# Two blocks on one core: the last VectorE chunk of the conditioning product moved into the feed forward's first up steps, the late pieces started one place earlier, the preparation's TensorE order restored

## The reference, cut to what matters

```python
def first_block(x, mem, ...):
    # rms_norm, projection, window attention + rwkv7 + memory attention
    x = x + concatenate([out_a, out_b, out_m], axis=-1) @ w_out[l]
    x = x + conv_ffn(rms_norm(x, ffn_norm_g[l]), w_up[l], conv_w[l], conv_b[l], w_down[l])

def second_block(x, c, w_ada, b_ada, ...):
    c_act = jax.nn.silu(c)
    mod = c_act @ w_ada[l] + b_ada[l]                 # 1024 x 6144: "conditioning"
    sh1, sc1, g1, sh2, sc2, g2 = jnp.split(mod, 6, axis=-1)
    h = rmsnorm(x, norm1_g[l]) * (1.0 + sc1) + sh1
    proj = h @ w_in[l]                                # queries and keys get a rotary turn
    ...                                               # two attentions, gates, w_out
    x = x + g1 * (merged @ w_out[l])
    h2 = rmsnorm(x, norm2_g[l]) * (1.0 + sc2) + sh2
    x = x + g2 * hierarchical_moe(h2, ...)            # 32 experts, 2 of them per token
```

## Time and profile before

| | us |
|---|---|
| median of the runs shown | 1062.68 |
| the profiled execution, its own time | 1064.43 |
| its span | 1062.6 |
| TensorE matmuls busy | 914.6 (86%) |
| VectorE busy | 551.4 (52%) |
| ScalarE busy | 358.7 (34%) |
| GpSimd busy | 76.1 (7%) |
| mean granted clock of TensorE | 0.944 |

### The profile page before, as it was taken

One profiled execution on the slowest core, in us unless ns is written; L12 is line 12 of the kernel. 1 busy time (PEld: TensorE's weight loads), 2 busy tenths in 40 slices (PEclk: granted clock), 3 DMA queues, 4 the chain that ended last, 5 costly groups with the idle time before them and its releaser, 6 DMA issues.

```text
span 1062.6 us, 19426 instructions
## 1 busy us (share of the span) xinstructions
PE 914.6 (86%) x8462; PEld 708.9 (67%) x8462; DVE 551.4 (52%) x1020; ACT 358.7 (34%) x699; POOL 76.1 (7%) x113
## 2 busy tenths in 40 slices
PE   9999999999999999999999998667665765657885
PEld 8777778489999888998989965334333343334532
DVE  4775688768888757798867543211112121112211
ACT  5710355156776545455553341000001010000002
POOL 3021710000000000331010000000000000000000
PEclk9999999999999999999999999989788788889978
DMA  9545353775554565886549899999999999999994
GB/s 346 168 140 188 144 210 105 261 253 169 164 163 171 204 226 206 266 246 204 179 157 391 348 389 429 428 429 428 430 428 429 428 427 430 429 428 429 427 431 175
DMA packets 76716, 316.21 MB, mean 298 GB/s; under 512 B 4088, under 2 KB 28065, under 8 KB 64209
## 3 DMA queue, kind: packets, MB, share of 16 engines
q1 hardware_dynamic: 71972, 302.24, 72.5%
q0 software_dynamic: 4512, 12.62, 3.9%
q10 hardware_dynamic: 140, 0.04, 0.0%
HBM read 311.72 MB, written 1.06 MB: 294 GB/s over the span
## 4 chain that ended last, share of the span: by engine, by line
PE 58%; DMA 26%; DVE 9%; issue 3%; ACT 2%; ACTq 0%; SPq 0%; POOL 0%; DVEq 0%
PE ps L486 56%; DMA w<-in_w_up 19%; DMA w<-in_w_gate 6%; DVE sp L1937 1%; DMA w<-in_w_ada 1%; DMA rot<-q 1%; PE ps L612 1%; PE ps L2800 1%; DVE w L1041 0%; DVE w L1003 0%; DVE acc L1003 0%; ACT hts L2934 0%; DVE rot L2308 0%; DVE q L2309 0%; DVE q L2311 0%
## 5 line engine op out<-in xcount | busy, mean ns | idle before, releaser
L486 PE MATMUL ps<-w,xg 128*32 128x256 f32 x2016 | 159.3, 475 | 96.9 <-DMA w<-in_w_up 74.1
L486 PE MATMUL ps<-hb,sp 128*128 128x256 f32 x1824 | 225.9, 285 | 0.0
L486 PEld LDWEIGHTS ps<-hb,sp 128*128 128x128 f32 x1824 | 220.1, 190 | 3.0 <-issue 2.5
L486 PEld LDWEIGHTS ps<-w,xg 128*32 128x32 f32 x2016 | 85.0, 132 | 169.1 <-issue 145.0
L1937 DVE TENSOR_TENSOR sp<-w,sp 128x1024 fp32r<-128x1024 f32 x122 | 144.7, 1221 | 38.6 <-ACT sp L1928 38.5
L1928 ACT ACTIVATE sp<-w 128x1024 fp32r<-128x1024 f32 x122 | 122.3, 1052 | 47.4 <-PE ps L486 46.2
L3010 DVE TENSOR_TENSOR cst<-ps,cst 64x256 f32<-64x256 f32 x31 | 13.3, 427 | 218.0 <-ACT cst L2921 218.0
L2921 ACT ACTIVATE cst<-ps 64x256 f32<-64x256 f32 x31 | 11.7, 377 | 313.2 <-PE ps L486 313.2
L3036 DVE TENSOR_TENSOR ost<-ps,cst 32x256 f32<-32x256 f32 x120 | 50.5, 420 | 102.5 <-PE ps L486 99.7
L486 PE MATMUL ps<-w,hts 128*32 128x256 f32 x1024 | 62.8, 386 | 11.9 <-ACT hts L2934 10.3
L486 PE MATMUL ps<-sp,ab 128*128 128x512 f32 x264 | 61.8, 395 | 0.0
(11 more groups left out here) (431 smaller groups left out, 1306.2 us busy)
## 6 DMA issues: line engine op xcount, KB each, us to landing
w<-in_w_down SPq DMA_DIRECT2D x36, 2048.0 KB, 35.8
w<-in_w_gate SPq DMA_DIRECT2D x32, 2048.0 KB, 28.1
w<-in_w_up SPq DMA_DIRECT2D x31, 2048.0 KB, 32.7
w<-in_w_in SPq DMA_DIRECT2D x13, 2048.0 KB, 9.9
w<-in_w_up SPq DMA_DIRECT2D x22, 1024.0 KB, 6.6
w<-in_w_ada SPq DMA_DIRECT2D x8, 2048.0 KB, 8.8
w<-in_w_out SPq DMA_DIRECT2D x4, 2048.0 KB, 8.2
w<-in_w_ada POOLq DMA_DIRECT2D x8, 768.0 KB, 5.6
```

What stands on the lines that cost most here:

```text
L486: return q.eng.matmul(o, l, r, start=start, stop=stop, skip_group_check=True)
```

## The change

It has three parts.

1. **Chunk 7.** `ada_ve(q, 7)` no longer runs between the additions of half 0. Its first four instructions stand behind the split of up half 2, the other four behind each of the next four splits (`up_ve`, i < 2). The activation blocks are numbered by `at_ab(n) = (n + 16) % 22`, so that the first six of them do not lie in slot 6.
2. **Late pieces.** `down_ve` begins with a `next(late_ada)`. GpSimd's program is as it was.
3. **Preparation.** On TensorE the head sums (`hsum_pe`) stand ahead of projection pair 3 and not within it; the sums' spread (`kk_pe`) and both halves of `feat_pe` (16 transposes) stand ahead of pair 4 and not within it.

```diff
+        def at_ab(n):
+            return (n + 16) % 22
...
-        def up_ve(q):
+        def up_ve(q, seventh):
             e = q.eng
             for i in range(11):
...
                 for z in range(2):
                     split_ve(q, 2 * i + z + 3)
+                    if i < 2:
+                        next(seventh, END)
...
         def down_ve(q, late_ada):
+            next(late_ada)
             for j in range(25, 33):
                 split_ve(q, j)
...
-            for i in (6, 7):
-                for _ in ada_ve(q, i):
-                    pass
-                wout_ve(q, 0, (i - 6,))
+            for _ in ada_ve(q, 6):
+                pass
+            wout_ve(q, 0)
+            seventh = ada_ve(q, 7)
...
             split_ve(q, 2)
-            up_ve(q)
+            two(seventh)
+            two(seventh)
+            up_ve(q, seventh)
...
+            hsum_pe(q, 0, HSB, [bsv[:, i, :] for i in range(3)], "hs", (s["r_kk"], 2))
             gates = lora_pe(q, 2)
             for n, _ in enumerate(rpair_steps(q, 3)):
-                if n == 1:
-                    hsum_pe(q, 0, HSB, [bsv[:, i, :] for i in range(3)], "hs", (s["r_kk"], 2))
                 if n in (1, 3, 5):
                     next(gates, END)
-            last = rpair_steps(q, 4)
             rq_pe(q, 0)
-            two(last)
             kk_pe(q)
-            for h in range(2):
-                two(last)
-                feat_pe(q, 1, Xm, lambda i: (s["ht1"], i + 5), hs=(h,))
-            two(last)
+            feat_pe(q, 1, Xm, lambda i: (s["ht1"], i + 5))
+            rpair_pe(q, 4)
```

More of the change, by code:

```diff
@@ L2018, in up_sc @@
                 q.wait_ge(s["u_v"], 9 * i + 9)
-                e.activation(ap_[0][:, 2 * i:2 * i + 2, :], Uc[:, 0:2, :], ACT.Copy).then_inc(s["a_hi"], 1)
-        def up_ve(q):
+                e.activation(ap_[0][:, at_ab(2 * i):at_ab(2 * i) + 2, :], Uc[:, 0:2, :], ACT.Copy).then_inc(s["a_hi"], 1)
+        def up_ve(q, seventh):
             e = q.eng
@@ L2035, in up_ve @@
                 q.wait_ge(s["a_hi"], i + 1)
-                e.tensor_tensor(ap_[1][:, 2 * i:2 * i + 2, :], Uc[:, 0:2, :], ap_[0][:, 2 * i:2 * i + 2, :].bitcast(F), SUB).then_inc(s["a_lo"], 1)
+                e.tensor_tensor(ap_[1][:, at_ab(2 * i):at_ab(2 * i) + 2, :], Uc[:, 0:2, :], ap_[0][:, at_ab(2 * i):at_ab(2 * i) + 2, :].bitcast(F), SUB).then_inc(s["a_lo"], 1)
         def ft3(i):
@@ L2051, in part @@
                         inside()
-                    t = mm3(q, psum[DB[2 * h + z]], [p[:, n, 128 * h:128 * h + 128] for p in ap_], [p[:, k, :] for p in w], n == 0, n == 21)
+                    t = mm3(q, psum[DB[2 * h + z]], [p[:, at_ab(n), 128 * h:128 * h + 128] for p in ap_], [p[:, k, :] for p in w], n == 0, n == 21)
                 return t
```

## The result

| | before | after |
|---|---|---|
| median of the runs, us | 1062.68 (five runs, 1060.68 to 1064.59) | 1094.17 (five runs, 1093.57 to 1096.69) |
| the profiled execution, its own time / its span | 1064.43 / 1062.6 | 1094.17 / 1092.4 |
| TensorE matmuls busy | 914.6 (86%) | 918.6 (84%) |
| mean granted clock | 0.944 | 0.935 |

The ratio is 1.0298, 95% interval 1.0286 to 1.0311: by this ratio the change makes the kernel 31.7 us slower. The forecast was 1088, in a range of 1076 to 1098. The mechanism was the one forecast; the sum was 6 us short.

What follows compares the result with a forecast made beforehand. The prediction took the experts' weight stream (DMA share nine tenths) to bound the kernel, delayed by work ahead, with VectorE on the chain in `proj2`. Terms -2.2 - 0.5 + 26.7 + 1 = +25 on 1062.68 gave 1088 us, range 1076 to 1098.

Steps and rivals of the forecast that it cites:

- the loop: In `proj2`, each late copy stands behind an exchange needing a rotary turn that stands behind the piece before; +26.7 us.
- The two signs in the preparation and at half 0: Both were forecast as gains: preparation -2.2 us, chunk 7 with half 0's additions -0.5 us.
- from half 4 on each exchange waits for a rotary turn: In `proj2`, the argument that late rotary turns hold the exchanges, given against the rival "The loop does not close".
- piece 10 in turn 43 adds 0.2 over piece 9 and finds its copy landed: Last link in `proj2`: VectorE, 26.5 us late at turn 36, loses only 0.2 us more at piece 10.
- The clock: TensorE idle times of 5 to 10 us in `proj2` lower its granted clock; +1 us, bounds 0 and +5.
- The gains: Preparation (-2.2 us) and chunk 7 (-0.5 us): TensorE waits less, and half 0's second addition comes sooner.
- The term for the preparation: TensorE's idle times of 0.47 and 2.12 us mostly go, against a new wait of about 0.6; -2.2 us, bounds 0, -2.6.
- Cost 0 for chunk 7's instructions in the up steps: Eight VectorE instructions (6.3 us) fit into idle time and the cover of three-deep split tiles; 0, without cover 2.1 us.
- for the step in the down product: The extra late-piece step (2.1 us) in the down product is covered the same way, at no cost there.
- The loop does not close: Rival in `proj2`: copies of pieces 7 to 9 issued at their old times, so slower but less; 1070 us, chance 0.07.
- VectorE is relieved: Rival in `proj2`: one 2.3 us piece leaves VectorE's stretch on the chain, TensorE waits 1.3 less; 1058.7 us, chance 0.04.

Runs made afterwards that it cites:

- experiment 1: Kernel before plus only the extra late-piece step at the start of the down product: 1096.42 us against 1062.2, ratio 1.0318.
- experiment 2: Changed kernel without the extra step in the down product: 1061.43 us against 1062.2 before, ratio 0.9991.
- experiment 3: Changed kernel with GpSimd's order of late pieces also moved ahead by one: 1060.55 us against 1062.2 before; repeated, 1061.87 against 1062.7.
- experiment 4: Changed kernel with the late piece of projection turn 3 left out, so later turns take their old pieces: 1060.43 us against 1062.75 before, ratio 0.9982.
- experiment 5: Changed kernel with only piece 6's copy started ahead of the exchange of half 2: 1089.91 us against 1062.75 before, ratio 1.0247.
- experiment 6: Changed kernel with only piece 10's copy started ahead of the exchange of half 9: 1087.11 us against 1062.75 before, ratio 1.0228.
- 7: Kernel before with only the chunk 7 part of the change: 1062.01 us against 1062.75, ratio 0.999.
- experiment 9: Kernel before with the extra down-product step and GpSimd's order moved ahead, without the other two parts: 1062.57 us against 1062.7, ratio 0.9996.
- experiment 10: As experiment 3, with late pieces of turns 35, 43, 51, 59 in turns 47, 51, 55, pieces 10, 11 started behind half 9's exchange: 1059.22 against 1062.7.

## Why the prediction was right, and where it was short

**What was right.** The sign, and the loop link by link up to piece 9. For pieces 6 to 9 the forecast gave the landings 443.1, 457.5, 473.9 and 496.4 on the clock of before. With the 3.96 us by which after's trace is ahead there, the waits ended at 441.1, 456.9, 474.0 and 496.1. Piece 6's copy took 5.1 and not 7.1, piece 7's 7.0 and not 6.0; the errors cancelled in part, which is luck. VectorE was 26.2 us late at turn 36, forecast 26.5. GpSimd's issue of piece 6 stood 2.0 us behind the exchange's release by ScalarE, as said. The waits of VectorE were said to be about 10, 6, 6 and 9 us, and were 9.39, 7.27, 6.43 and 8.62; TensorE's idle times of 5 us or more came at four places and not three, the fourth (517.22) for piece 10; the first expert copy came 30.1 us later and not 24; the stage from the first expert copy on is as long as before (508.7 against 509.0). The two signs in the preparation and at half 0 held as well. One link was put too simply: "from half 4 on each exchange waits for a rotary turn" holds for halves 4 to 7, while the exchanges of halves 8 and 9 waited for ScalarE. Experiments 1 to 5 bear out the cause: the line alone gives the loss (1), the order alone removes it (3), the step without the shift is free (4), and no cascade explains it (5).

**The step that failed** is "piece 10 in turn 43 adds 0.2 over piece 9 and finds its copy landed". It waited 5.63 us. Two things were overlooked. The copy of piece 10 stands behind the exchange of half 9, as each copy before it stood behind an exchange, and that exchange waited for ScalarE until 501.05. And the copy took 10.07 us instead of the median of 5.2. With 5.2 it would have landed at 508.2 against 507.5 when VectorE was free for it, a wait of 0.7; had it been started when piece 9 was done, none (experiment 6). So the two together made the price. The queue had been followed link by link to piece 9, and the last link was taken as free because the pieces' places lie further apart there. The range of 1076 to 1098 had no term for this: its upper 7 us were for four longer copies, pieces 6 to 9, and the clock's bound of 5 went into it only in part. That 1094.17 still lies inside is luck as much as judgement.

**The clock** was sized at 1, for the waits ahead of pieces 6 to 9. There it cost next to nothing: up to piece 10, VectorE's own idle times (32.3 us more than before) account for the whole delay (32.2). The 1.5 us that it did cost (experiment 6) stand behind the wait for piece 10, which the forecast did not have. So the size came near for another reason than the one given.

**The gains** were sized at 2.7, and the trace of after seemed to show 4. The runs show less: 1.0 for both parts (experiment 2, -0.3 to 2.2), 1.9 with the step kept (experiment 4, 0.3 to 3.5). The term for the preparation left out the wait of 0.92 for L846, which the head sums met in their new place, and the slow clock behind the new wait for L1313, which costs 1.4 to 1.7 us in six of the nine traces with this order. The old order had a slow stretch in two of four traces, so how much of the gain this takes is not known. Cost 0 for chunk 7's instructions in the up steps, and for the step in the down product, was borne out within these intervals (7 and 4).

**The sum by the runs:** 33.8 for the step (experiment 1) less 1.0 to 1.9 for the rest is 31.9 to 32.8; measured 31.7. The trace of after agrees: 32.2 up to piece 10 and 1.5 of clock behind it are 33.7. Without the link at piece 10 it is 24.2 (experiment 6), where the forecast of 25 had left that link out.

**The rivals.** "The loop does not close" (1070) would have shown the exchange of half 4 released by ScalarE; it was released by `DVE q L2318`. "VectorE is relieved" (1058.7) needed another order on GpSimd. With that order (experiment 3) the time is 1.9 to 2.0 under before, and the 1.3 us that the relief should bring did not show by itself (experiment 9). It took two pieces out of the stretch to collect it (experiment 10).

## What to carry to other kernels

A generator that hands out steps on one engine and a hand-written order on another are one schedule: who takes one step more on the first must follow the second's queue, copy by copy, to its end, and must not stop at the last link but one. A step that costs nothing where it is put can cost its whole chain where its successors stand. And a gain of 2 or 3 us between two single traces is within what two executions of the same kernel differ by; ask for it a kernel that is unchanged up to that point.

## What the runs showed of the hardware that was not expected

- **A copy of 768 KB from GpSimd's queue took 10.07 us** after (503.03), 10.37 in experiment 1, and 10.2 in experiment 5 (issued at 500.87, wait ended at 511.09), where the other copies of that size on the chain took 4.8 to 7.0. In the windows from 502 to 510 the DMA share was 1.02 and 1.03, with a copy of 2 MB of `w_in` that SyncE had issued at 500.10; in the windows 486 to 490 and 490 to 494, while piece 9 was copied in 4.8 us, it was 0.55 and 0.36. The Trainium skill ("DMA: Bandwidth & Descriptors", Anatomy of one DMA) has 2.0 us and the bytes over 436 GB/s, an estimate of 3.8 us; no copy of that size on this chain came down to it, and the longest was 2.7 times as long. That the other queue's transfers make it long fits the shares, but was not tried by itself.
- **The clock after waits.** It was 1.00 in all three windows of 20 us from 444 to 504 before. After, between the waits, the windows of 20 us from 440 on have 0.87, 0.70, 0.83 and 0.91. Up to piece 10 VectorE or a copy held the chain, and the slow clock cost next to nothing; behind the last wait, where TensorE was on the chain, it cost 1.5 us (experiment 6).
- **Scatter in the early stages.** The same kernel twice (experiment 3 and its repeat) differed by 1.2 us at 66 us, by 2.35 us at 404 us and by 3.8 us in the span. The first of these is the granted clock: behind the same wait of 0.48, the 16 transposes took 1.94 us in one execution and 3.54 in the other.
